# Index dots and sliding-window logits: the three passes of two heads issued in turn, one head in each half of the rows

## The reference

```python
# layer one, per block of 128 queries
dots = jnp.einsum('bqjd,bsd->bqjs', qib, k_idx) * (IDX_DIM ** -0.5)
score = jnp.einsum('bqj,bqjs->bqs', wib, jax.nn.relu(dots)).astype(jnp.float32)
...
# layer two
logits = jnp.einsum('bnqkgd,bnskd->bnkgqs', q, kk).astype(jnp.float32) * (Dh ** -0.5)
```

## Time and profile before

| what | value |
|---|---|
| timed runs: median (lowest to highest) | 1253.8 us (1253.1 to 1254.78), 3 runs |
| the profiled execution: span | 1252.3 us |
| PE busy | 1192.8 us, 95% of the span |
| DVE / ACT / POOL busy | 638.1 / 467.7 / 573.3 us |
| mean granted PE clock | 0.989 |

### The profile page before, as it was taken

How to read it: one execution, slowest core, us unless ns; L and a number is a source line. 1 busy time by engine, 2 the same in 40 slices (tenths; PEclk the granted TensorE clock), 3 DMA queues, 4 the chain that set the end, 5 groups by cost and what they waited for, 6 DMA issues and landing times.

```text
span 1252.3 us, 16936 instructions
## 1 busy us (share of the span) xinstructions
PE 1192.8 (95%) x5580; PEld 976.2 (78%) x5580; DVE 638.1 (51%) x1095; ACT 467.7 (37%) x872; POOL 573.3 (46%) x336
## 2 busy tenths in 40 slices
PE   5999988889999999999999999899999999999996
PEld 4757877668888888888888778788888888888885
DVE  5458989995554444442222368846644444431111
ACT  4243146765333223333222367643333322232222
POOL 4333476663444444443444464304444444444441
PEclk9999999999999999999999999899999999999998
DMA  5712321102333333333333342303233333323331
GB/s 161 248 36 68 120 60 39 39 29 77 94 101 100 100 96 87 88 88 92 93 92 103 101 111 59 68 1 101 79 91 100 100 100 100 90 70 93 92 92 67
DMA packets 178709, 110.37 MB, mean 88 GB/s; under 512 B 7425, under 2 KB 173372, under 8 KB 178668
## 3 DMA queue, kind: packets, MB, share of 16 engines
q1 hardware_dynamic: 178224, 108.69, 30.4%
q10 hardware_dynamic: 444, 1.16, 0.3%
HBM read 107.70 MB, written 6.33 MB: 91 GB/s over the span
## 4 chain that ended last, share of the span: by engine, by line
PE 85%; DVE 8%; issue 3%; DMA 1%; ACT 1%; POOL 0%; DVEq 0%; ACTq 0%; SPq 0%
PE ps L608 28%; PE ps L610 27%; PE ps L609 27%; DVE prob L1547 1%; PE ps L781 1%; DVE raw L1547 1%; DMA q_all<-in_x 1%; DVE b_prob L1742 1%; DVE prob L1569 1%; DVE ss L1437 1%; DVE xs_lo L1380 1%; DVE raw L1569 1%; DVE xs_lo L1424 1%; PE ps L938 1%; DMA raw<-in_b_w_in 0%
## 5 line engine op out<-in xcount | busy, mean ns | idle before, releaser
L480 POOL TENSOR_TENSOR w_lo<-raw,w_hi 128x1024 fp32r<-128x1024 f32 (+1 forms) x200 | 462.8, 2335 | 560.2 <-ACT w_hi L1033 560.1
L608 PE MATMUL ps<-xs_hi,w_hi 128*128 128x512 f32 x960 | 380.2, 396 | 5.5 <-DVE x L1420 3.7
L609 PE MATMUL ps<-xs_lo,w_hi 128*128 128x512 f32 x960 | 374.3, 390 | 0.0
L610 PE MATMUL ps<-xs_hi,w_lo 128*128 128x512 f32 x960 | 374.2, 390 | 0.0
L1033 ACT CAST w_hi<-raw 128x1024 fp32r<-128x1024 f32 (+1 forms) x200 | 183.0, 964 | 470.2 <-PE ps L610 457.8
L608 PEld LDWEIGHTS ps<-xs_hi,w_hi 128*128 128x128 f32 x960 | 180.6, 188 | 50.9 <-issue 6.1
L610 PEld LDWEIGHTS ps<-xs_hi,w_lo 128*128 128x128 f32 x960 | 180.5, 188 | 37.9
L609 PEld LDWEIGHTS ps<-xs_lo,w_hi 128*128 128x128 f32 x960 | 180.7, 188 | 37.3 <-issue 1.2
L608 PE MATMUL ps<-act_hi,w_hi 128*128 128x512 f32 x352 | 139.2, 396 | 0.0
L610 PE MATMUL ps<-act_hi,w_lo 128*128 128x512 f32 x352 | 138.0, 392 | 0.0
L609 PE MATMUL ps<-act_lo,w_hi 128*128 128x512 f32 x352 | 136.6, 388 | 0.0
(11 more groups left out here) (191 smaller groups left out, 1568.6 us busy)
## 6 DMA issues: line engine op xcount, KB each, us to landing
raw<-in_ffn_w_gate_up SPq DMA_DIRECT2D x88, 512.0 KB, 4.9
raw<-in_ffn_w_down SPq DMA_DIRECT2D x32, 384.0 KB, 3.6
raw<-in_a_w_in SPq DMA_DIRECT2D x21, 512.0 KB, 4.6
raw<-in_ffn_w_down SPq DMA_DIRECT2D x32, 320.0 KB, 4.0
raw<-in_b_w_in SPq DMA_DIRECT2D x10, 512.0 KB, 5.1
bias_toep<-bias_row SPq DMA_DIRECT2D x1, 4096.0 KB, 19.2
toep<-bias_toep SPq DMA_DIRECT2D x16, 256.0 KB, 2.6
raw<-in_a_w_out SPq DMA_DIRECT2D x8, 512.0 KB, 4.0
```

The costliest lines, as they stand in the source:

```text
L480: nc.gpsimd.tensor_tensor(pieces(w_lo, n)[half], pieces(raw, n)[half], pieces(w_hi, n)[half].bitcast(F32), ALU.subtract)\
L608: nc.tensor.matmul(dst, wh, xh, start=start, stop=False, **kw)
L609: nc.tensor.matmul(dst, wh, xl, start=False, stop=False, **kw)
L610: return nc.tensor.matmul(dst, wl, xh, start=False, stop=stop, **kw)
```

## The change

A new helper, `mm3_two`, issues the three passes of two heads in turn: first pass of head 0, first pass of head 1, second of head 0, and so on. In the index dots it takes heads j and j + 1 together, and the two projection `mm3` follow behind the pair. The waits are those of the later head, and `dots` is raised by two at the end of the pair. In layer two it takes the two heads of a pair together for each block i; the loop over a is gone, both heads of a bank number b are announced together (`blg_done` by two), and DVE waits for both.

```diff
--- before.py
+++ after.py
@@ -609,6 +609,14 @@
                 nc.tensor.matmul(dst, wh, xl, start=False, stop=False, **kw)
                 return nc.tensor.matmul(dst, wl, xh, start=False, stop=stop, **kw)
 
+            def mm3_two(dst, wh, wl, xh, xl):
+
+
+                for w, x, first, end in ((wh, xh, True, False), (wh, xl, False, False), (wl, xh, False, True)):
+                    for u in range(2):
+                        last = nc.tensor.matmul(dst[u], w[u], x[u], start=first, stop=end)
+                return last
+
             def tile(dst, n, it, col, ncol, rhs_hi, rhs_lo, k0=0, nk=DM, start=True, stop=True):
 
 
@@ -696,21 +704,24 @@
                 pe.wait_ge(qa_done, h + 1)
 
                 pe.wait_ge(lo_done, 2 * n + 2)
-                for j in range(JI):
+                for j in range(0, JI, 2):
                     d = h * JI + j
                     if d >= 4:
 
-                        pe.wait_ge(relu_done, d - 3)
+                        pe.wait_ge(relu_done, d - 2)
                     if d < 4:
 
-                        pe.wait_ge(qi_l, d + 1)
-                    r = slice(DH * (j % 2), DH * (j % 2) + DH)
-                    mm3(ps[:, (d + 2) % 4, 0:(i + 1) * P], qi_hi[r, j // 2, i * P:(i + 1) * P],
-                        qi_lo[r, j // 2, i * P:(i + 1) * P], ki_hi[r, 0:(i + 1) * P],
-                        ki_lo[r, 0:(i + 1) * P], True, True).then_inc(dots, 1)
-                    c = j * 256 + (h % 2) * P
-                    last = mm3(ps[:, 4 + h % 2, :], w_hi[:, n % 2, c:c + P], w_lo[:, n % 2, c:c + P],
-                               xh(j), xl(j), j == 0, j == DM - 1)
+                        pe.wait_ge(qi_l, d + 2)
+                    r = (slice(0, DH), slice(DH, P))
+                    n_keys = (i + 1) * P
+                    mm3_two([ps[:, (d + u + 2) % 4, 0:n_keys] for u in range(2)],
+                            [qi_hi[q, j // 2, i * P:(i + 1) * P] for q in r],
+                            [qi_lo[q, j // 2, i * P:(i + 1) * P] for q in r],
+                            [ki_hi[q, 0:n_keys] for q in r], [ki_lo[q, 0:n_keys] for q in r]).then_inc(dots, 2)
+                    for k in (j, j + 1):
+                        c = k * 256 + (h % 2) * P
+                        last = mm3(ps[:, 4 + h % 2, :], w_hi[:, n % 2, c:c + P], w_lo[:, n % 2, c:c + P],
+                                   xh(k), xl(k), k == 0, k == DM - 1)
                 last.then_inc(unit_done, 1)
 
             pe.wait_ge(csq_done, 1)
@@ -953,24 +964,23 @@
                 if 2 <= k < DM + 2:
                     h2 = k - 2
                     b_turn(h2, 0, k)
-                for a in range(2):
-                    if k < DM:
-                        if a == 0:
-
-                            pe.wait_ge(bql_done, k + 1)
-                        r = slice(a * DH, (a + 1) * DH)
-                        for b in range(2):
-                            if k >= 1:
-
-                                pe.wait_ge(bneg_done, 8 * (k - 1) + 4 * a + 2 * b + 2)
-                            for i in (2 * b, 2 * b + 1):
-                                n = P if i == 0 else 2 * P
-                                c0 = (0, P, 0, 2 * P)[i]
-                                k0 = max(i - 1, 0) * P
-                                last = mm3(ps[:, 2 * a + b, c0:c0 + n], bq_hi[r, par, i * P:(i + 1) * P],
-                                           bq_lo[r, par, i * P:(i + 1) * P], bk_hi[r, k0:k0 + n],
-                                           bk_lo[r, k0:k0 + n], True, True)
-                            last.then_inc(blg_done, 1)
+                if k < DM:
+
+                    pe.wait_ge(bql_done, k + 1)
+                    r = (slice(0, DH), slice(DH, P))
+                    for b in range(2):
+                        if k >= 1:
+
+                            pe.wait_ge(bneg_done, 8 * (k - 1) + 4 + 2 * b + 2)
+                        for i in (2 * b, 2 * b + 1):
+                            n = P if i == 0 else 2 * P
+                            c0 = (0, P, 0, 2 * P)[i]
+                            k0 = max(i - 1, 0) * P
+                            last = mm3_two([ps[:, 2 * a + b, c0:c0 + n] for a in range(2)],
+                                           [bq_hi[q, par, i * P:(i + 1) * P] for q in r],
+                                           [bq_lo[q, par, i * P:(i + 1) * P] for q in r],
+                                           [bk_hi[q, k0:k0 + n] for q in r], [bk_lo[q, k0:k0 + n] for q in r])
+                        last.then_inc(blg_done, 2)
                 if 2 <= k < DM + 2:
                     b_turn(h2, 1, k)
                 if k in Q_OF_STEP:
@@ -1711,7 +1721,7 @@
                             n = P if i == 0 else 2 * P
                             c0 = (0, P, 0, 2 * P)[i]
 
-                            dve.wait_ge(blg_done, 4 * k + 2 * a + i // 2 + 1)
+                            dve.wait_ge(blg_done, 4 * k + 2 * (i // 2) + 2)
                             dve.wait_ge(bbias_done, 2 * k + a + 1)
 
                             dve.wait_ge(bsink2_done, 4 * k + 4)
```

## The result

The changed kernel takes 1238.8 us (median of four runs, 1238.4 to 1239.7) beside 1253.9 for the kernel before (four runs on the same chip): a ratio of 0.988, interval 0.9866 to 0.9890, so 15.1 us or 1.2% less. Forecast were 1239.4 us. Its profiled execution has a span of 1236.8 us, 2.0 us under the median.

The account below looks back on a forecast made before the run. TensorE was taken as the bound (85% of the chain of waits). Dots 10.4 plus logits 4.0 make 14.4 us off the 1252.3 span, giving 1237.9; plus 1.5 to the median, 1239.4 us, range 1236 to 1243.

Parts of the forecast that it names:

- Steps (1) and (2): Index dots: alternating halves, each pair takes the time of one head, with one round trip per pair; 11.2 us saved.
- Step (3): End of the dots: DVE finishes later against PE, so PE stands 0.8 us (0 to 1.7) for `c_nrm`.
- Step (4): Layer two's logits: twelve pairs replace 24 passes; at most 9.3 us, of which 4.0 arrive after waits for DVE.
- the clock: Whole kernel: a shifted window of half clock can move the forecast or any rival by 1 to 2 us.
- Nothing given back: Rival, dots and layer two: neither the 0.8 us nor the waits in the logits are lost; 1233.3 us, chance 0.12.
- DVE takes all of layer two: Rival, layer two's attention: DVE takes back the whole gain of the logits; 1243.4 us, chance 0.15.
- No sustained overlap: Rival, dots and logits: only 12 round trips saved (5.0 us), layer two loses its overlap (3.1); 1251.9 us, chance 0.08.
- A drain per change of half: Rival, dots and logits: each change of half drains the array, 0.21 us each, 236 more; 1302 us, chance 0.04.
- The attribution of `b_bm`'s late start to a fetch: Layer two, steps 0 to 2: `b_bm` waits for a table fetch queued behind 1 MB of weights; gain only 0.3 us.

Follow-up runs that it names:

- e4: Changed kernel with both heads of a dots pair read from the first 64 partitions and layer two's logits as before the change; 1250.95 us (one run).
- e3: Changed kernel with dots pairs issued as three passes of one head, then three of the other, and logits as before the change; 1243.6 us, ratio 0.9922.
- e5: Changed kernel with the dots of the kernel before and logits issued three passes of one head, then three of the other; 1248.5 us (one run).
- e6: Changed kernel with the dots of the kernel before and logits issued in runs of six passes per head; 1251.7 us (one run).
- e1: Changed kernel with only the index dots changed, layer two's logits loop as in the kernel before; 1244.0 us, ratio 0.9920.
- e2: Changed kernel with only layer two's logits changed, index dots as in the kernel before; 1250.5 us, ratio 0.9968.
- e12: Changed kernel with POOL splitting its weight slab before adding the bias table in the turn of pair 2; 1236.3 us, ratio 0.9859.
- e10: Changed kernel with DVE doing head 0's `bpt_lo` first in each layer-two step, ahead of sink copies and `bo_lo`; 1241.7 us, runs in two clusters.
- e9: Changed kernel with dots of four heads instead of two per round trip; 1238.9 us, ratio 0.9882.
- e7: Kernel before the change with four of POOL's `w_lo` splits cut to two subtractions over 8 columns each; 1246.9 us, ratio 0.9942.
- e8: Changed kernel with four of POOL's `w_lo` splits cut to two subtractions over 8 columns each; 1229.7 us, ratio 0.9802.

## Why the prediction was right

The forecast was 1239.4, the measurement 1238.8. Step by step:

- **Steps (1) and (2), overlap and round trips.** Right in both sizes. The stretch of dots is 27.65 us (27.7 expected), the periods 2.1 and 2.3 us, as reckoned. Counted the same way the stretch was 38.63 us before, not 38.9, so 11.0 us were saved and not 11.2. e4 separates the terms: 4.8 us for the round trips (5.0), 6.2 for the overlap (6.2). What the prediction put wrong is the reason for the overlap. It said that it comes because passes alternate; e3 and e5 have it with three passes of a head in a row, and e6, with six in a row, has 9 of 12 pairs. Which half the rows are in decides (e4), and how far ahead the partner is.
- **Step (3), the wait for `c_nrm`.** The right wait at the right place; 0.55 us instead of 0.8. DVE's lag behind PE grew by 1.66 us (0.69 to 2.35), where 1.7 were reckoned. Four relus (at 68.85, 69.44, 70.03 and 86.78) waited on DVE, none did before; the prediction put that at nothing, and it had no effect on PE. 11.0 - 0.55 is 10.4 us, against 10.5 measured at the transposes, where 0.25 is a dots stretch that began earlier, and 10.8 in e1's time.
- **Step (4), what arrives of 9.3 us.** By the starts of the steps, each measured against step 0, steps 0 to 2 gave 0.02 us (0.3 forecast): 0.41 were there at the start of step 2, and step 2, with a new stretch of half clock from 740.8 behind a step 1 in which PE idled, lost them. Step 3 gave 0.35 (0.3), step 4 1.0 (1.0), step 5 0.07 (0), step 6 0.51 (0.5). Step 7 gave 2.3 until its second transposes (1.9), since the last part of its logits ran at full clock again (2.20 us from first to last start, where the kernel before needs 4.39), and a further 0.8 came behind them, where the half clock of the kernel before lasted on. Together 5.1, where 4.0 were forecast. The waits for DVE and the steps without gain came as reckoned. What was off is the clock, by about +1.2 us in step 7 and -0.3 in step 2; the prediction had named it as a risk of 1 to 2 us and had put nothing in the sum.
- **The sum.** By the trace 10.4 + 5.1 = 15.5 us, by the times 15.1. The excess of 1.1 us over the forecast 14.4 is partly eaten by the distance from span to median, 2.0 us instead of 1.5. That the total is right to 0.6 us is luck in part; the terms are right to about 1 us each. The start of step 0 alone moves by up to 1.5 us among kernels with the same dots: 719.83 to 721.16 with the change (721.16 in the changed kernel itself), 730.04 to 731.58 without it.
- **Nothing given back** falls by the waits for `c_nrm` and `bpt_lo`. **DVE takes all of layer two** falls by e2, which gains 4.3 us with the logits alone. **No sustained overlap** falls by twelve pairs in a row, those of 256 columns at 0.119 us, with the two starts of a pair within 10 ns. **A drain per change of half** falls by the same rows: with 23 changes in a step the logits take the 1.39 us of their twelve pairs, which leaves no room for it.
- The page of the Trainium skill that the prediction set against itself, "TensorE: Matmul & The Clock Gate" (Part 1, "Wait — 56ns, not 53.3ns?"), puts the sequencer at about 62 ns per MATMUL with hardware decode off. Two passes would then take 124 ns. They take 119 ns here (0.83 us for the seven steps from 749.55 to 750.38), so that limit did not bind. No row says whether hardware decode was off.
- The prediction pointed to the earlier trace rows for DVE standing still, but those rows list POOL alone. What shows it are the rows of DVE at the end of this document, and e12.
- The attribution of `b_bm`'s late start to a fetch is borne out by the row above (733.03, DMA `b_toep`) and by e12, which took the split out from behind it and gained 2.6 us in that step. For the kernel before, the row at 743.44 names DVE; but this `b_bm` starts 11.9 us after the start of step 0 in both kernels, although step 1 begins 1.0 us sooner after it in the changed one, which speaks for the fetch. That the fetch is late because it is queued behind 1 MB of weights was not tested.

Open stay the two times of e10, and why the stretches of half clock fall where they do. In the attention of layer two they come to 10.2 us in all in the kernel before, in e1 and in the changed kernel, to 17.0 in e4 and e10, 13.6 in e9, 6.8 in e12, 3.4 in e7 and none in e8. No experiment held them fixed, so part of the difference between two kernels' times can be theirs.

## What to carry to other kernels

Where products over 64 rows stand between products over 128, put both halves' products into one stretch: here each saved round trip was worth 0.40 us (4.8 us for twelve), and the overlap halved the time of the passes. The order in the stretch made no difference here as long as no more than three passes of one half stood in a row; with six in a row the logits of a step took 1.74 us instead of 1.39. Then look at what DVE has to deliver behind the stretch: e9 saved 2.5 us of PE more and gave 2.4 of it back in two waits. Once PE waits for DVE while POOL holds it up, look for POOL work that is queued behind a fetch that it doesn't need (e12).

## What the runs showed of the hardware

- Passes over 64 rows on different halves start ahead of passes that were issued earlier: the first passes of the two heads start within 10 ns, with two passes issued between them (e3). Three passes find a partner per change of half in e6 (1.74 us a step; three changes, 0.34 us each) and in the kernel before (2.42; one change).
- A round trip from 128 rows to 64 and back costs 0.40 to 0.42 us, whether three passes on one half lie in it (before), six on one half (e4) or six on two (after).
- Weight loads of the two halves don't disturb each other: a pair of passes over 256 columns takes 0.119 us, loads included (0.83 us for seven, from 749.55), as one pass does alone (0.83 us for seven in the kernel before, from 733.17).
- Beside POOL's `w_lo` and `b_bm`, one normalisation of `b_prob` on DVE took as long as the operation of POOL that ran with it, and ended just behind it: 0.81 and 0.84 us beside the two `b_bm` (0.74 each), 2.45 and 2.43 beside the two halves of `w_lo` (2.41 and 2.39). The four took 6.30 us from 733.04, and four more 1.08 us from 739.66, where POOL was still. DVE's reductions, which read PSUM, were not held (0.48 us beside `w_lo` in e12):

```profile
733.04 6.30 DVE L1752 TENSOR_SCALAR b_prob<-b_prob,b_rinv 128x128 f32<-128x128 f32 x4
...
739.66 1.08 DVE L1752 TENSOR_SCALAR b_prob<-b_prob,b_rinv 128x128 f32<-128x128 f32 x4
```
